# Moving the MLP's weight slots and activation tiles by multiples of 64 and 32 bytes in on-chip memory

## The reference

```python
for layer in range(DEPTH):
    u = rmsnorm(h, norm_mix_pre[layer])
    ...                       # f = u @ w_in; mixer; mix = o @ w_out
    h = h + rmsnorm(mix, norm_mix_post[layer])
    u = rmsnorm(h, norm_ffn_pre[layer])
    ff = jnp.square(jax.nn.relu(u @ w_ffn_up[layer])) @ w_ffn_down[layer]
    h = h + rmsnorm(ff, norm_ffn_post[layer])
```

## Time and profile before

| | |
|---|---|
| median of 3 runs | 1567.32 us (1565.9 to 1569.51) |
| span of the profiled execution | 1565.6 us |
| PE busy | 1492.0 us, 95% of the span, 9901 matmuls |
| VectorE, ScalarE, GpSimd busy | 844.8, 666.4, 91.4 us |
| TensorE clock granted, mean | 0.981 of full speed |
| DMA | 119.38 MB, mean 76 GB/s |

### The profile page before, as it was taken

How to read it: one execution, slowest core, us unless ns; L and a number is a source line. 1 busy time by engine, 2 the same in 40 slices (tenths; PEclk the granted TensorE clock), 3 DMA queues, 4 the chain that set the end, 5 groups by cost and what they waited for, 6 DMA issues and landing times.

```text
span 1565.6 us, 24908 instructions
## 1 busy us (share of the span) xinstructions
PE 1492.0 (95%) x9901; PEld 1243.9 (79%) x9901; DVE 844.8 (54%) x1400; ACT 666.4 (43%) x1156; POOL 91.4 (6%) x132
## 2 busy tenths in 40 slices
PE   5999998999999999999999997999989999999997
PEld 4776776887778888878888986988868888878886
DVE  4366546777676442334436626787746442334433
ACT  5543434445545442124334434676645442124331
POOL 0110013322300000000000002000000000000000
PEclk8999999999999999999999998999999999999999
DMA  6222200000152233322331241000042323322321
GB/s 224 81 70 78 81 14 14 2 2 2 55 189 76 99 94 110 95 81 94 108 122 55 81 139 64 2 2 3 2 135 68 93 93 110 95 81 94 108 81 54
DMA packets 32607, 119.38 MB, mean 76 GB/s; under 512 B 3696, under 2 KB 3824, under 8 KB 32496
## 3 DMA queue, kind: packets, MB, share of 16 engines
q1 hardware_dynamic: 29808, 108.84, 21.7%
q10 hardware_dynamic: 2688, 8.98, 1.6%
HBM read 115.71 MB, written 2.10 MB: 75 GB/s over the span
## 4 chain that ended last, share of the span: by engine, by line
PE 74%; DVE 8%; ACT 3%; issue 1%; DMA 0%; ACTq 0%; DVEq 0%; SPq 0%
PE bank L337 19%; PE bank L339 18%; PE bank L338 18%; PE bank L2543 2%; PE bank L2556 2%; PE bank L1136 2%; PE bank L2532 1%; PE bank L2533 1%; PE bank L1118 1%; PE bank L1082 1%; PE bank L2135 1%; DVE nmax L2613 1%; PE bank L1022 1%; PE bank L1126 1%; DVE ul_m L459 1%
## 5 line engine op out<-in xcount | busy, mean ns | idle before, releaser
L330 DVE TENSOR_TENSOR wl_m<-ring,wh_m 128x1024 fp32r<-128x1024 f32 x124 | 152.0, 1226 | 158.5 <-ACT wh_m L322 156.2
L337 PE MATMUL bank<-uh_m,wh_m 128*128 128x512 f32 (+2 forms) x576 | 216.5, 376 | 3.6 <-DVE ffo L1946 1.9
L338 PE MATMUL bank<-ul_m,wh_m 128*128 128x512 f32 (+2 forms) x576 | 216.0, 375 | 0.0
L339 PE MATMUL bank<-uh_m,wl_m 128*128 128x512 f32 (+2 forms) x576 | 216.0, 375 | 0.0
L322 ACT ACTIVATE wh_m<-ring 128x1024 fp32r<-128x1024 f32 x124 | 131.6, 1061 | 192.2 <-PE bank L339 189.7
L337 PE MATMUL bank<-wh_m,hh 128*128 128x512 f32 x448 | 174.4, 389 | 0.0
L338 PE MATMUL bank<-wl_m,hh 128*128 128x512 f32 x448 | 174.3, 389 | 0.0
L339 PE MATMUL bank<-wh_m,hl 128*128 128x512 f32 x448 | 174.3, 389 | 0.0
L1936 DVE TENSOR_TENSOR hraw<-hraw 128x512 f32<-128x512 f32 x64 | 44.3, 693 | 166.7 <-ACT hraw L1892 166.6
L1892 ACT ACTIVATE hraw<-bank 128x512 f32<-128x512 f32 x64 | 38.3, 598 | 214.8 <-PE bank L339 214.8
L337 PEld LDWEIGHTS bank<-uh_m,wh_m 128*128 128x128 f32 x576 | 108.6, 189 | 24.9 <-issue 2.7
(11 more groups left out here) (418 smaller groups left out, 2809.1 us busy)
## 6 DMA issues: line engine op xcount, KB each, us to landing
ring<-in_wstream_dram SPq DMA_DIRECT2D x200, 512.0 KB, 3.5
rowbuf<-in_rows_dram ACTq DMA_DIRECT2D x6, 512.0 KB, 3.8
xres<-in_x_dram SPq DMA_DIRECT2D x4, 512.0 KB, 6.7
xres<-in_x_dram ACTq DMA_DIRECT2D x1, 2048.0 KB, 10.0
out_dram<-xres ACTq DMA_DIRECT2D x4, 512.0 KB, 4.5
prerow<-in_rows_dram ACTq DMA_DIRECT2D x3, 512.0 KB, 4.9
con<-in_consts_dram SPq DMA_DIRECT2D x1, 869.5 KB, 13.3
par<-in_params_dram SPq DMA_DIRECT2D x1, 680.5 KB, 11.7
```

What stands on the lines that cost most here:

```text
L330: v.sig(v.e.tensor_tensor(dn[3][:, c % RING, :], slot(c), dn[2][:, c % RING, :].bitcast(F32), ALU.subtract), sem("w_lo"), it * per + c + 1)
L337: pe.matmul(out, lh, rh, start=start, stop=False)
L338: pe.matmul(out, lh, rl, start=False, stop=False)
L339: return pe.matmul(out, ll, rh, start=False, stop=stop)
```

## The change

The two weight rings get 16 float32 (64 bytes) more for each slot, so that slot c starts 64 c bytes further than before modulo 512. A ring then has 4 x 4160 = 16640 = 32 x 512 + 256 bytes, so that `wl_m` starts at 256. The filler `apart` shrinks to 896 x 4 = 3584 = 7 x 512 bytes, which puts `uh_m` at 0, and 32 bytes are put between `uh_m` and `ul_m`, which puts `ul_m` at 32. The filler `gap3` of layer 1 grows by 512 bytes, which moves the attention's tiles behind it by 512. No instruction, wait, loop or transfer is added, removed or moved; only addresses change.

```diff
-        wh_m, wl_m = (sb(n, [P, RING, D], F32R, c=ml) for n in ("wh_m", "wl_m"))
+        wh_m = sb("wh_m", [P, RING, D + 16], F32R, c=ml)[:, :, 0:D]
+        wl_m = sb("wl_m", [P, RING, D + 16], F32R, c=ml)[:, :, 0:D]
         ffo = sb("ffo", [P, NT, D], c=ml)
         prerow = sb("prerow", [P, D], c=ml)
         hraw = sb("hraw", [P, 2, T], c=ml)
-        sb("apart", [P, 1120], c=ml)
-        uh_m, ul_m = (sb(n, [P, KD, T], F32R, c=ml) for n in ("uh_m", "ul_m"))
+        sb("apart", [P, 1024 - 128], c=ml)
+        uh_m = sb("uh_m", [P, KD, T], F32R, c=ml)
+        sb("stagger", [P, 8], c=ml)
+        ul_m = sb("ul_m", [P, KD, T], F32R, c=ml)
...
-        sb("gap3", [P, 64], c=l1)
+        sb("gap3", [P, 64 + 128], c=l1)
```

## The result

The changed kernel takes 1571.52 us (median of 20 runs, 1569.01 to 1574.16), the kernel before 1567.32 us (20 runs, 1565.60 to 1571.83). The ratio is 1.0022, with a 95% interval from 1.0015 to 1.0029: slower by about 0.2%, so little that single runs of the two overlap. The forecast was 1572.0 us. The profiled execution of the changed kernel has a span of 1568.6 us.

A forecast was written before the change was run, and what follows sets the result against it. The matrix engine's step from one matmul start to the next was taken to bound the MLP; +6.2 + 1.3 - 1.2 - 0.8 - 0.3 - 0.4 = +4.8 us gave 1572.0 us, range 1558 to 1577.

The forecast's parts named there:

- the balance: MLP: three down slots in four lose alignment, +6.2 us; slot 0 of the up product lines up, -1.2 us.
- The modulus: Offsets between moving row and stationary piece were taken modulo 512 bytes; 256 was priced 6 ns slower than 0.
- The price at 64: A matmul step at offset 64 was priced 230 ns, against 226.6 at 0, from one single step.
- the rule that each matmul has its own price and a train their mean: Each step was priced by its own offset and averaged: up slot 0 -3.7 ns, the other up slots unchanged.
- The pair that meets: In the matmul trains, the moving row's read was paired with the load of the next matmul's stationary piece.
- The small terms: Layer 1's input projection +1.3 us, down chunks in `uh_m` -0.8, output projections -0.3 with `wh_m` and -0.4 with `wo`.
- rows 5 to 7: Profile rows of fast steps: down product, start of one loop, layer 0's projection; their mean priced offset 0 at 226.6 ns.
- Aligned enough: Rival: a slot's 64 c is harmless, every dense step takes 226.6 ns; -11.4 us, 1555.9 us; chance 0.27.
- No lock: Rival: each chunk's new offset keeps even slot 0 slow, settling needs about 24 steps; +12.4 us, 1579.7 us; chance 0.11.
- It cancels: Rival: fast slots of the up and down products balance; no change, 1564 to 1570.5 us; chance 0.14, shared with "Offsets are not the cause".
- Offsets are not the cause: Rival: ports are independent, something else separates fast from slow steps; 1564 to 1570.5 us; chance 0.14, shared with "It cancels".
- rule of the Trainium skill: Matrix engine has two independent SBUF read ports and never waits on anyone; by it time stays at 1567.3 us.

The follow-up runs named there:

- experiment 2: Kernel before with only the slots shifted as in the change, `uh_m` and `ul_m` left at 384: 1569.41 us beside 1568.49, ratio 1.0007.
- experiment 3: Kernel before with slots shifted by 256 bytes instead of 64, all else at offset 0: 1557.37 us beside 1568.49, ratio 0.9934.
- Experiment 8: Kernel before with everything at offset 0 except `ul_m`, 32 bytes further: 1564.59 us in a single run, beside 1568.71.
- experiment 4: Kernel before with unshifted slots, `wh_m` and `uh_m` at 0, `wl_m` and `ul_m` at 128: 1577.95 us in a single run, beside 1568.49.
- experiment 9: The change without its 32 bytes, so `ul_m` at 0; beside the kernel before: 1568.57 against 1567.74 us, ratio 1.0005.
- experiment 5: experiment 4 with the second and third product of `mm3` exchanged: 1566.23 us in a single run, beside 1568.71 for the kernel before.
- experiment 1: Kernel before with only filler `apart` cut from 1120 to 1024 floats, moving `uh_m` and `ul_m` to 0: 1559.30 us beside 1568.49, ratio 0.9936.
- experiment 6: experiment 1 plus 112 floats that bring `wo` from 64 to 0; beside the kernel before: 1558.35 against 1568.71 us, ratio 0.9924.
- experiment 7: Kernel before with slots 32 bytes apart (0, 32, 64, 96), everything else at 0: 1571.67 us in a single run, beside 1568.71.

## Why the prediction was right, and where its steps were not

**Right.** That the matrix engine alone sets the time in the MLP, and that the change acts by addresses only: the counts are unchanged, the splits still take 1226 and 1061 ns as in the earlier trace rows, and the steps account for +4.3 us. The groups of the two splits in the changed kernel (busy us, mean ns | idle):

```profile
L333 DVE TENSOR_TENSOR wl_m<-ring,wh_m 128x1024 fp32r<-128x1024 f32 x124 | 152.0, 1226 | 161.4 <-ACT wh_m L325 159.1 <-DVE hl L1942 0.5
L325 ACT ACTIVATE wh_m<-ring 128x1024 fp32r<-128x1024 f32 x124 | 131.6, 1061 | 196.6 <-PE bank L342 194.1
```

Right too is the balance. The down product loses more than the up product gains: +5.6 and -1.6 us against +6.2 and -1.2 in the sum. The down group was to rise to 393 or 394 and is at 394; slot 0 there was to stay at 227 to 229 ns (227.4 in the row, 227.9 on the mean), slots 2 and 3 were to show 232 to 234 (232.8 and 233.4).

**The modulus.** The prediction took 512, called it its choice, and so priced 256 and 320 like any other offset. Experiments 2 and 3 show that 256 is free. In the down product, slot 0 thus lost 0.8 ns where 2.0 were predicted, all of it in the first five steps of a chunk, a start-up cost that the sum didn't have, and slot 1 lost 3.1 where 4.3 were; slots 2 and 3 lost 6.1 and 6.7 where 6 was taken for both. The price at 64, 3.4 ns from a single step of the attention, was near: 2.7 to 3.1 in whole trains.

**The up product: total right, parts wrong.** -3.7 ns were predicted for slot 0 and nothing for the others; measured are -0.9, +0.7, -3.2 and -1.3. The step that failed is the rule that each matmul has its own price and a train their mean. Experiment 8 shows that one row in three off its place makes all three steps slow, and experiment 4 that it can cost as much as if all were off. So slot 0, with `ul_m` 32 bytes off, gained little; without the 32 bytes it has 227.4 ns (experiment 9). Why slot 2 (offsets 128, 160, 128 modulo 256) gains most is not explained. That the sum of the four came out near was partly luck.

**The pair that meets.** The moving row against the piece loaded next was read from two starts at the same time. Experiment 4 contradicts it, and experiment 5 shows that the order counts without saying how. What is shown: a train whose rows and pieces all stand at one place modulo 256 is fast. In uniform trains, with one offset for all three lines, the step is 226.7 ns at 0 (up to 228.5 on the mean of a chunk that comes behind one at another offset), 229.4 to 229.8 at 64, 232.3 to 232.8 at 128, 233.2 to 233.5 at 192. The mechanism under it stays open.

**The small terms.** The chunks in `uh_m` gained 0.4 us instead of 0.8, the output projections 0.2 instead of 0.7, and the input projection lost 0.9 instead of 1.3; for the chunks the reason is the 32 bytes, as experiments 8 and 9 show (231.8 with them, 227.4 without). They explain the output projection with `wo` as well (229.6 without them, 231.8 in the change), but not the one with `wh_m` (232.7 without, 232.2 with). Two slips of the sum are too small to matter: the mean of rows 5 to 7 is 226.5 ns, not 226.6, and 1567.3 + 4.8 is 1572.1 us, not 1572.0.

**The rivals.** *Aligned enough* fails, since the up slots are not at 226.6 and the down slots are no longer. Its price was sound: it gave -11.4 us for all products lined up, and the medians of experiments 1, 3 and 6, where all or all but `wo` are, lie 9 to 11 us lower. *No lock* has its outcome in slot 0 of the up product alone (231.7), and there by the 32 bytes. Its mechanism exists but is short: trains behind another offset do settle, in five steps of slot 0 of the changed down product and nine in experiment 7, not 24. *It cancels* fails, since the products don't balance: +5.6 against -1.6 us. *Offsets are not the cause* falls with experiment 1: one filler, -0.64%. With it falls, for these steps, half of the rule of the Trainium skill that the prediction set against itself (SBUF — State Buffer, section Who interferes with whom): by it the matrix engine's two read ports are independent, and steps of one shape differ here by 7 ns with the places of their operands. The other half, that it waits for no other engine, agrees with the up steps of the kernel before, 232.6 ns with and without other engines at work.

## What to carry to other kernels

Where a stretch is bound by the matrix engine, look at the step from one start to the next in the timeline, not at the share of busy time or the mean duration: 100% busy hid steps that were 6 ns, or 2.6%, too long, and a filler of another size gave most of that back. With operands like these, put the moving rows and stationary pieces of one train of matmuls at one offset modulo 256 bytes, ring slots included, and measure every stagger: in the lined-up kernel each shift that was tried and was no multiple of 256 cost time. A forecast from offsets can have the right total while its pieces are wrong, so test one offset at a time.

## What the runs showed of the hardware

- The step of a 128x512 fp32r matmul with a weight load of its own lies, on the mean of a slot, between 226.7 and 233.9 ns at full clock, with the relative byte offsets of what it reads.
- The pattern repeats after 256 bytes (256: 226.5 to 227.2 ns), and inside it a shift by 32 is worse than one by 64: 233.5 against 229.4 ns in the down product.
- One operand of three that is 32 bytes off slows the whole train: 232.6 against 226.7 ns.
- A train at offset 0 behind a chunk at another offset has slow steps first, and then 226.7 ns: of 24 the first five in the change (231.0 ns on the mean, 230.0 in the chunk shown), the first nine in experiment 7 (231.1).
- The order of the three products, at equal addresses, changes the step by 2.2 ns when their offsets are mixed (231.1 to 228.9).
